# A hybrid decoder step on one core: the fourth expert of each group of four multiplied down by column quarters

## The reference

```python
def expert_block(args):
    xblk, e = args
    return (jax.nn.silu(xblk @ w_gate[e]) * (xblk @ w_up[e])) @ w_down[e]

yb = lax.map(expert_block, (xb, block_e)).reshape(n_slots, d) * slot_w[:, None]
return jax.ops.segment_sum(yb, slot_tok, num_segments=n_tok + 1)[:n_tok]
```

## Time and profile before

| what | value |
|---|---|
| three runs | 1441.70, 1441.41, 1439.46 us; median 1441.41 |
| profiled execution, its own time | 1440.47 us |
| its span in the profile | 1438.6 us, 1.87 us less |
| TensorE busy | 1256.8 us, 87% |
| bytes moved | 503.61 MB, 350 GB/s over the span |

### The profile page before, as it was taken

How to read it: one execution, slowest core, us unless ns; L and a number is a source line. 1 busy time by engine, 2 the same in 40 slices (tenths; PEclk the granted TensorE clock), 3 DMA queues, 4 the chain that set the end, 5 groups by cost and what they waited for, 6 DMA issues and landing times.

```text
span 1438.6 us, 19986 instructions
## 1 busy us (share of the span) xinstructions
PE 1256.8 (87%) x8413; PEld 650.3 (45%) x8413; DVE 450.5 (31%) x887; ACT 223.1 (16%) x465; POOL 44.8 (3%) x30
## 2 busy tenths in 40 slices
PE   8999999999999998997787777887788777778777
PEld 7888888888788862231222222222222122222222
DVE  4322127674211142332321321331232232233142
ACT  3111232322000033110011011011001001111101
POOL 0000003140000001000000000000000000000000
PEclk9999999999999999999998999899899999999899
DMA  9975443669399349999999999999999999999997
GB/s 342 348 222 183 141 132 121 207 203 340 89 349 409 119 164 428 417 428 430 433 428 436 427 433 436 427 434 431 430 436 427 433 436 426 436 428 426 430 429 308
DMA packets 101729, 503.61 MB, mean 350 GB/s; under 512 B 9470, under 2 KB 79750, under 8 KB 85302
## 3 DMA queue, kind: packets, MB, share of 16 engines
q1 hardware_dynamic: 89618, 494.37, 84.6%
q10 hardware_dynamic: 12068, 8.63, 1.9%
HBM read 496.42 MB, written 6.59 MB: 350 GB/s over the span
## 4 chain that ended last, share of the span: by engine, by line
PE 55%; DMA 41%; DVE 2%; ACT 1%; issue 1%; SPq 1%; ACTq 0%; DVEq 0%
PE bank L702 30%; DMA ring<-in_w_gate 16%; DMA ring<-in_w_up 14%; DMA ring<-in_w_down 10%; PE bank L981 9%; PE bank L1018 4%; PE bank L916 2%; PE bank L1036 2%; DMA ring<-in_w_in 1%; PE bank L1033 1%; PE bank L1055 1%; DVE xa L1830 1%; PE bank L1049 1%; PE bank L998 0%; PE bank L793 0%
## 5 line engine op out<-in xcount | busy, mean ns | idle before, releaser
L702 PE MATMUL bank<-bc,ring 128*128 128x264 f32 x1536 | 350.9, 387 | 1.9 <-ACT cat L1186 1.3
L981 PE MATMUL bank<-ring,bc 128*32 128x512 f32 x2040 | 268.2, 659 | 89.5 <-DMA ring<-in_w_gate 58.5
L702 PEld LDWEIGHTS bank<-bc,ring 128*128 128x128 f32 x1536 | 288.1, 190 | 52.4 <-issue 2.3
L1830 DVE TENSOR_TENSOR xa<-xa,bank 128x512 f32<-128x512 f32 x192 | 119.8, 682 | 243.5 <-PE bank L1036 196.0
L981 PEld LDWEIGHTS bank<-ring,bc 128*32 128x32 f32 x2040 | 63.2, 117 | 264.5 <-issue 153.4
L702 PE MATMUL bank<-cat,ring 128*128 128x264 f32 x512 | 116.0, 387 | 0.0
L702 PEld LDWEIGHTS bank<-cat,ring 128*128 128x128 f32 x512 | 96.6, 190 | 19.0 <-issue 2.9
L1844 DVE COPY bc<-bank 128x512 f32<-128x512 f32 x32 | 22.1, 691 | 210.3 <-PE bank L981 210.3
L1018 PE MATMUL bank<-ring,cat 128*32 128x512 f32 x480 | 66.4, 674 | 19.9 <-DMA ring<-in_w_down 19.7
L916 PE MATMUL bank<-cat,bc 128*32 128x512 f32 x512 | 61.3, 597 | 13.5 <-DVE xa L1830 13.5
L1018 PE MATMUL bank<-ring,xa 128*32 128x512 f32 x512 | 62.3, 607 | 6.3 <-DMA ring<-in_w_down 4.1
(11 more groups left out here) (286 smaller groups left out, 981.9 us busy)
## 6 DMA issues: line engine op xcount, KB each, us to landing
ring<-in_w_gate SPq DMA_DIRECT2D x24, 4096.0 KB, 31.2
ring<-in_w_up SPq DMA_DIRECT2D x24, 4096.0 KB, 31.3
ring<-in_w_down SPq DMA_DIRECT2D x24, 4096.0 KB, 32.6
ring<-in_w_in SPq DMA_DIRECT2D x23, 2048.0 KB, 13.9
ring<-in_w_up SPq DMA_DIRECT2D x16, 2048.0 KB, 22.9
ring<-in_w_gate SPq DMA_DIRECT2D x15, 2048.0 KB, 28.9
ring<-in_w_down SPq DMA_DIRECT2D x13, 2048.0 KB, 28.7
ring<-in_w_out SPq DMA_DIRECT2D x8, 2048.0 KB, 16.5
```

The lines of the kernel that those rows point to most:

```text
L702: m = pe.matmul(bank[n % 3][:, 0:T], w[:, k, (i % TPU) * P:(i % TPU + 1) * P], src[:, k, :], start=n_k == 0, stop=n_k == KT - 1)
L981: m = pe.matmul(bank[b][c * C:(c + 1) * C, :], xeT[j % 2][:, k, :], wx, start=i == 0 and x < 4, stop=i == 1 and x >= 4, skip_group_check=True)
L1830: V.tensor_tensor(xa[:, t, cols], xa[:, t, cols], bank[to[n]][:, :], ALU.add).then_inc(mix_added, 1)
```

## The change

In every group the fourth expert's down product, the mixing of the third and the fourth, and the stores after the last group are made anew.

- `end_products(q)` computes one quarter of the output columns at a time: the four column groups now hold the four chunks of contraction c, so that `bank[2]` has four partial sums of quarter q on its four groups of partitions. There are four rounds of four matmuls, as before, but each round ends a quarter.
- ScalarE copies each quarter's partial sums to `g_sb` or `u_sb` in turn. `mix_last(q)` mixes them with `gateT3`, a copy of the fourth expert's turned weights in `xa`: one matmul with all 128 rows of contraction adds the four partial sums while it mixes. There are three for each quarter (t = 0, 1, 2).
- `mix_second_last(t, q)`, the third expert's mixing, opens the same banks (`END_BANKS`), and `mix_last` accumulates on it, so VectorE adds each bank once for both experts (11 additions in the order of `END_ADD`).
- Tile t = 1 has no `residual` any more, except for the last quarter, which keeps the identity matmul (line 1167 of the new file) and ScalarE's copy (line 1453).
- `turn_gate(3)` comes earlier, right after `turn_rows` of the fourth expert.
- In the last group the last 4 MB are issued when both halves of their place in the ring have been used: columns 0 to 1023 in one transfer of 2 MB (pieces of 4 KB), then quarters 2 and 3 with 1 MB each (pieces of 2 KB). Before, a piece was 16 KB or, for the two last halves, 8 KB. TensorE waits for the first two quarters together, for the third and for the fourth.
- SP stores quarter q of both prompt tiles and of the sample rows as soon as it is added, while TensorE works on the next.

```diff
+END_STEPS = [(t, q) for q in range(3) for t in (0, 1, 2)] + [(t, 3) for t in (2, 0, 1)]
+END_MIX = {s: n + 1 for n, s in enumerate(END_STEPS)}
+END_ADD = {s: n + 1 for n, s in enumerate(x for x in END_STEPS if x != (1, 3))}
+NEND = len(END_ADD)
+END_BANKS = {0: (5, 0, 3, 5), 1: (7, 1, 4, 7), 2: (6, 6, 6, 6)}
...
+                    src = wd[NG - 1, :, EG - 1, :].rearrange("p (c d) -> p c d", c=FC)
+                    to = ring[:, s:s + 2, :].rearrange("p a (c d) -> p (a c) d", c=FC // 2)
+                    sp.dma_start(to[:, :, 0:1024], src[:, :, 0:1024]).then_inc(slot_full[s], 16)
+                    sp.sem_inc(slot_full[s + 1], 16)
+                    for q in (2, 3):
+                        cols = slice(512 * q, 512 * q + 512)
+                        sp.dma_start(to[:, :, cols], src[:, :, cols]).then_inc(end_in[q - 2], 16)
...
+            for q in range(3):
+                cols = slice(512 * q, 512 * q + 512)
+                sp.wait_ge(end_added, every + END_ADD[(1, q)])
+                sp.dma_start(y[:, :, cols], xa[:, 0:2, cols]).then_inc(y_stored, 16)
+                sp.wait_ge(end_added, every + END_ADD[(2, q)])
+                sp.dma_start(ys[:, cols], xa[q * C:q * C + NB, 2, 0:512]).then_inc(y_stored, 16)
+            cols = slice(1536, 2048)
+            sp.wait_ge(end_added, every + END_ADD[(2, 3)])
+            sp.dma_start(ys[:, cols], xa[3 * C:3 * C + NB, 2, 0:512]).then_inc(y_stored, 16)
+            sp.wait_ge(end_added, every + END_ADD[(0, 3)])
+            sp.dma_start(y[:, 0, cols], xa[:, 0, cols]).then_inc(y_stored, 16)
...
+                def mix_second_last(t, q):
+                    rows_ = slice(q * C, (q + 1) * C)
+                    pe.matmul(bank[END_BANKS[t][q]][:, :], gateT[rows_, t, :], ye[rows_, :],
+                              start=(t, q) != (1, 3), stop=False, skip_group_check=True)
+                def end_products(q):
+                    if q == 0:
+                        pe.wait_ge(ye_copied, it * (EG - 1) + EG - 1)
+                        end_weights[:] = [weights("d", EG - 1, i).rearrange("p (c d) -> p c d", c=FC // 2) for i in range(2)]
+                    else:
+                        pe.wait_ge(end_copied, it * 4 + q)
+                    if q >= 2:
+                        pe.wait_ge(end_in[q - 2], it * 16 + 16)
+                    for c in range(FC):
+                        m = pe.matmul(bank[2][c * C:(c + 1) * C, :], actT[(EG - 1) % 2][:, c, :],
+                                      end_weights[c // 2][:, c % 2, q * 512:(q + 1) * 512], start=True, stop=True, skip_group_check=True)
+                        if (q, c) == (3, 1):
+                            m.then_inc(down_half, 1)
+                    m.then_inc(down_done if q == 3 else end_down, 1)
+                def mix_last(q):
+                    pe.wait_ge(end_copied, it * 4 + q + 1)
+                    for t, q_ in END_STEPS:
+                        if q_ != q:
+                            continue
+                        if t == 2:
+                            m = pe.matmul(bank[END_BANKS[2][q]][q * C:(q + 1) * C, :], gateT3[:, 2, 0:C], (g_sb, u_sb)[q % 2],
+                                          start=False, stop=True, skip_group_check=True)
+                        else:
+                            m = pe.matmul(bank[END_BANKS[t][q]][:, :], gateT3[:, t, :], (g_sb, u_sb)[q % 2],
+                                          start=False, stop=True, skip_group_check=True)
+                        m.then_inc(end_mixed, 1)
...
                     if j == EG - 1:
-                        residual(0)
-                        residual(1)
-                        residual(3)
+                        pe.wait_ge(gateT_copied, e)
+                        turn_gate(EG - 1)
                     if j >= 2:
                         adds_done((2, j - 2))
                     down(j - 1, 0, e)
                     turn_hidden(e)
-                    if j == EG - 1:
-                        residual(2)
                     down(j - 1, 1)
 
                 e = it * EG + EG - 1
+                pe.wait_ge(act_ready, e + 1)
+                end_products(0)
+                pe.wait_ge(gateT_copied, e + 1)
                 pe.wait_ge(xe_ready, 2 * e + 4)
...
-                pe.wait_ge(ye_copied, e)
-                pe.wait_ge(gateT_copied, e)
-                mix_part((0, EG - 2), 0)
-                mix_part((0, EG - 2), 1)
-                pe.wait_ge(act_ready, e + 1)
-                mix_part((0, EG - 2), 2).then_inc(mixed, 1)
-                for n in range(4):
-                    mix_row(EG - 2, n)
-                adds_done((0, EG - 2), -2)
-                mix_part((0, EG - 2), 3).then_inc(mixed, 1)
-                mix((2, EG - 2))
-                adds_done((0, EG - 2), -1)
-                turn_gate(EG - 1)
-                down(EG - 1, 0)
-                down(EG - 1, 1)
-                pe.wait_ge(ye_copied, e + 1)
-                pe.wait_ge(gateT_copied, e + 1)
-                adds_done((2, EG - 2))
-                mix((0, EG - 1))
-                for n in range(4):
-                    if n == 3:
-                        adds_done((0, EG - 1), -3)
-                    mix_row(EG - 1, n)
-                mix((2, EG - 1))
+                for t in (0, 1):
+                    for q in range(3):
+                        mix_second_last(t, q)
+                for q in range(4):
+                    rows_ = slice(q * C, (q + 1) * C)
+                    pe.matmul(bank[END_BANKS[2][q]][rows_, :], gateT[rows_, 2, 0:C], ye[rows_, :],
+                              start=True, stop=False, skip_group_check=True)
+                end_products(1)
+                mix_last(0)
+                end_products(2)
+                mix_last(1)
+                pe.wait_ge(end_added, it * NEND + (NEND + END_ADD[(1, 0)]))
+                pe.matmul(bank[END_BANKS[1][3]][:, :], ident, xa[:, 1, 1536:2048], start=True, stop=False, skip_group_check=True)
+                mix_second_last(1, 3)
+                mix_second_last(0, 3)
+                end_products(3)
+                mix_last(2)
+                mix_last(3)
...
+                for q in range(4):
+                    if q < 3:
+                        act.wait_ge(end_down, it * 3 + q + 1)
+                    else:
+                        act.wait_ge(down_done, it * EG + EG)
+                    if q >= 2:
+                        act.wait_ge(end_mixed, it * len(END_MIX) + 3 * (q - 1))
+                    A((g_sb, u_sb)[q % 2], bank[2][:, :], ACT.Copy).then_inc(end_copied, 1)
+                act.wait_ge(end_mixed, it * len(END_MIX) + END_MIX[(1, 3)])
+                A(xa[:, 1, 1536:2048], bank[END_BANKS[1][3]][:, :], ACT.Copy).then_inc(row_moved, 1)
...
+                    for t, q in END_ADD:
+                        dve.wait_ge(end_mixed, it * len(END_MIX) + END_MIX[(t, q)])
+                        rows_ = slice(q * C, (q + 1) * C) if t == 2 else slice(0, P)
+                        cols = slice(0, 512) if t == 2 else slice(q * 512, (q + 1) * 512)
+                        V.tensor_tensor(xa[rows_, t, cols], xa[rows_, t, cols], bank[END_BANKS[t][q]][rows_, :], ALU.add
+                                        ).then_inc(end_added, 1)
```

107 lines of the change are left out of this document (37 added, 70 removed).

## The result

| | before | after |
|---|---|---|
| time, median of 5 runs each on one chip, us | 1440.2 | 1451.7 (1447.48 to 1452.03) |
| profiled execution / its span, us | 1440.5 / 1438.6 | 1451.7 / 1449.5 |
| last matmul to end of span, us | 6.05 | 3.35 |

The change makes the kernel slower: ratio 1.0066, 95% interval 1.0055 to 1.0078, that is 9.5 us by the ratio. The forecast was 1448.0 us with a range of 1443.6 to 1451.0: right in sign, 3.7 us short of the profiled run and the median, which lie 0.7 us above the range. The ratio, taken on the median that the forecast started from (1441.41 us), gives 1450.9 us, which lies inside it.

A forecast was written before the change was run, and what follows sets the result against it. The weight stream sets the pace until the last weights, then TensorE and stores: start 1420.6 + tail 20.2, copy to 1441.4, end 2.9, clock 1.7 gives span 1446.0; 1.87 over span and 0.1 give 1448.0 us, range 1443.6 to 1451.0.

The forecast's parts named there:

- The removed identity matmuls are worth nothing: Ahead of the fourth's down: their time turns into TensorE waits of 2.2 and 3 us for weights.
- Start of the tail: Last group, when the first two quarters' weights land and TensorE's new tail begins: 1420.6 us (1420.3 to 1421.4).
- the pieces: Smaller transfer pieces of the first 2 MB of the last weights: 0.3 us later landing, bounds 0 to 1.1.
- TensorE's tail: TensorE's rounds from the first quarter's product to its end in the last group: 20.2 us, ending at 1440.8 us.
- the rival in which full-array mixings overlap: The fourth's 12 mixings run four deep, 3 us instead of 10.1, giving 1439.1 us at full clock; chance 0.05.
- The clock: First rounds of the last group's tail at half clock after two close waits: 1.7 us, up to 3.4; chance 0.55.
- The end: Behind ScalarE's last copy at 1441.4 us, last two stores to the end of the span: 2.9 us (2.4 to 3.6).
- the stores in between gain nothing by themselves: Stores of earlier quarters at the kernel's end: neither cost nor gain; only the last quarter's are late.
- The groups before: Earlier groups' tails grow by 2 us in the first, 4 to 7 in later ones, at no cost.
- The 12 us of cover: In earlier groups an issue may come 12 us later before the stream stops; beyond that, the excess counts seven times.
- The range: Whole kernel: 1443.6 to 1451.0 us, leaving out better packing, overlap, the dry stream and a bit of each side.
- The rival with larger pieces' cost: Tail starts 0.8 us later, with stores and clock at their upper ends: 1450.5 us; chance 0.06.

The follow-up runs named there:

- e6: Kernel before with only the new cut of the last 4 MB, all of it waited for ahead of the fourth's down: 1442.78 us, ratio 1.0013.
- e1: Changed kernel with its two waits filled by 9 and 13 small unread matmuls in every group: 1448.41 us, ratio 1.0050 to the kernel before.
- e8: Changed kernel with e2's order and nine fill matmuls ahead of the third's second down half: 1445.91 us, ratio 1.0039 to the kernel before.
- e3: Changed kernel with the fourth's mixing of prompt tokens cut to the first 128 of each 512 columns: 1448.52 us, ratio 1.0044 to the kernel before.
- e12: Changed kernel with six 512-column matmuls at the start of every group but the first: 1450.12 us, ratio 1.0066 to the kernel before.
- e4: Changed kernel with all of SP's stores held back until the last addition: 1456.43 us, ratio 1.0099 to the kernel before.
- e7: Kernel before with turn_gate early, two identity matmuls moved into waits, and the fourth's mixing in three rounds: 1440.51 us, ratio 1.0000.
- e9: Kernel before with six overwritten 512-column matmuls at the start of every group but the first: 1441.21 us, ratio 1.0001.
- e5: Kernel before with 24 overwritten 128 x 128 matmuls at the start of every group but the first: 1451.51 us, ratio 1.0076.
- e11: Kernel before with 24 overwritten matmuls of 8 columns at the start of every group but the first: 1458.44 us, ratio 1.0121.
- e10: Kernel before with sixteen overwritten 512-column matmuls at the start of every group but the first: 1456.54 us, ratio 1.0110.
- e2: Changed kernel with the third's mixing placed ahead of the first quarter's product: 1447.02 us, ratio 1.0035 to the kernel before.

## Why the prediction was right, and where it was off

- *The removed identity matmuls are worth nothing.* Right: waits of 2.20 and 2.54 us (forecast 2.2 and 3).
- *Start of the tail.* 1421.31 us, forecast 1420.6, bound 1421.4. The stream was 0.5 us late already from the second group on. The rest, 0.2 us, may be the pieces, but e6's trace gives them no cost: there the first 2 MB land at 1419.8 us.
- *TensorE's tail.* 20.2 us at full clock was right: e1 measures 20.4 us (1422.44 to 1442.83). Eleven rounds in place of three are the largest part of why the change is slower, 10.5 us in e8 against 4.05 before; e3 shows that they are on the path, e8 that 5.6 us stay when both waits are filled, and the rival in which full-array mixings overlap is out. No run gave the changed kernel its three rounds back.
- *The clock.* This is the term that was mis-sized: 1.7 us, measured 4.4 us in the profiled execution (e1 against the changed kernel), over its bound of 3.4; over all executions the ratios of the two give 2.3 us. I had the two waits as the cause, and filling them takes it away. But I counted with a low stretch that ends soon after the wait; it lasted 9.5 us into a tail in which TensorE never paused. In e12 it cost 1.5 us behind the same waits, so whether 1.7 came out was in part luck. With start, tail and clock TensorE ends 3.7 us later than forecast, which is the whole miss.
- *The end.* 2.7 us from the end of ScalarE's copy to the end of the span, forecast 2.9. But "the stores in between gain nothing by themselves" was wrong: e4 puts them at 4.8 us. The sum was not hurt, since it took the end with only the last stores outstanding; the sentence should have said that this is what they buy. I had read the kernel before's end as the issue of four small stores; e7's trace shows the 2 MB of stores beside it, about 6 us from the first store on.
- *The groups before.* Right that they cost nothing: e9 (0.1 us for 5.4 us more) and e12. The 12 us of cover from the earlier trace rows fit e5, where 14.0 us added lost 1.5 a group. Others fit less well: in e11 19.0 us were added and about 2.5 a group lost, and in the last groups of e10 13.9 us were added and nothing was lost. What is lost is not simply the excess over 12, and that stays open.
- *The range.* The rival with larger pieces' cost was summed too low: 0.8, 0.7 and 1.7 us on 1448.0 are 1451.2 us, not 1450.5. The range's upper end of 1451.0 so cut into a case that was written down, and the median of 1451.7 lies just above both.
- *What is not settled.* Why the clock stays low for 13.6 us in three traces (the changed kernel, e3 and e4), 6.8 us in e2 and 3.4 us in e12. None of the runs varied this alone.

## What to carry to other kernels

Behind the last transfer, count TensorE's rounds, not its instructions: partial sums of 128 rows need as many rounds as there are tiles, and four products of 32 rows side by side need a quarter. Early stores are worth something (here 4.8 us), but not when the matmuls that make them possible take 10 us more. And put behind a waiting instruction only what needs the same data: moving work that was ready ahead of the wait was worth 4.5 us together with the shorter half clock, half of what the change lost.

## What the runs showed of the hardware that was not expected

- The granted clock stayed at 0.50 for 9 us with TensorE busy 8.69 of them (36 records, among them products and mixings of 512 columns). Being busy again did not bring the 2.4 GHz level back at once, and how long it took differs between builds with nearly the same waits: 9.5 us of work in the changed kernel, 3.3 us in e12.
- Added instructions can cost more than their time. 24 short matmuls in the kernel before brought 87 instruction packets and a standstill of 4.2 to 5.4 us in six groups of seven; 6 wide ones of the same total time brought none, and 32. Sixteen wide ones lay between: 51 packets, a standstill in two groups of seven. In the changed kernel 22 short ones (e1) brought 33 packets. Where the limit lies was not measured.
- The issue of a transfer can take very long. The last piece of 1 MB, cut into lines of 2 KB, held its queue for 19.93 us, where the issues before it took 0.65 and 1.68 us:

```profile
1392.74 19.93 SPq L620 DMA_DIRECT2D ring<-in_w_down  x1
```

In the kernel before such an issue took 0.43 us. e6 has the same (21.64 us for two). The landing was not delayed by it in e6 (1425.1 us against 1425.3 before); in the changed kernel the last piece lands at 1426.3 us, 1.0 us later than before, where the first 2 MB were 0.8 us late already. Nothing else was due on SP's queue in the changed kernel before 1433 us.
